# Token rows loaded in a second layout, and the normalizing root moved behind the first projection

## The reference

```
h = rmsnorm(x, g)        # x * rsqrt(mean(x*x) + eps) * g, row by row
z = h @ w_in             # columns [q_a | k_a | v_a | q_b | k_b | v_b | g_b | gate_a | gate_b]
q_b, k_b = rope(q_b), rope(k_b) * DK**-0.5
```

## Time and profile before

| | us |
|---|---|
| median of 3 runs (2119.41 to 2120.04) | 2119.41 |
| the profiled execution | 2120.73 |
| its span, first to last instruction | 2118.9 |
| PE busy / DVE / ACT / POOL | 1940.3 / 1164.1 / 852.5 / 211.5 |
| stage A, tile 0: from the start to the first transposes of q and k | 39.25 |
| stage A, tiles 1 to 8: from there to the same place of tile 8 | 145.12 |

### The profile page before, as it was taken

How to read it: one execution, slowest core, us unless ns; L and a number is a source line. 1 busy time by engine, 2 the same in 40 slices (tenths; PEclk the granted TensorE clock), 3 DMA queues, 4 the chain that set the end, 5 groups by cost and what they waited for, 6 DMA issues and landing times. The chain is left out here.

```text
span 2118.9 us, 26600 instructions
## 1 busy us (share of the span) xinstructions
PE 1940.3 (92%) x9596; PEld 1570.7 (74%) x9596; DVE 1164.1 (55%) x1459; ACT 852.5 (40%) x1018; POOL 211.5 (10%) x222
## 2 busy tenths in 40 slices
PE   6999999974999999997998998689999999999498
PEld 5888888863777777765887786577778777778386
DVE  4234333315333444324444434589999999997574
ACT  4232000011333343324222212477777777776342
POOL 0000111122000000000222000100000000000220
PEclk9999999987999999998999998899999999999699
DMA  8445111187687756584333436589999999997552
GB/s 304 163 154 221 45 57 64 42 295 281 234 309 284 248 177 227 191 290 169 134 128 106 161 110 258 193 323 393 397 396 392 392 391 393 393 397 303 211 193 84
DMA packets 123894, 503.52 MB, mean 238 GB/s; under 512 B 16816, under 2 KB 32688, under 8 KB 101040
## 3 DMA queue, kind: packets, MB, share of 16 engines
q1 hardware_dynamic: 111808, 462.42, 58.5%
q0 software_dynamic: 7200, 26.22, 3.4%
q10 hardware_dynamic: 4816, 13.96, 1.7%
HBM read 407.66 MB, written 94.90 MB: 237 GB/s over the span
## 5 line engine op out<-in xcount | busy, mean ns | idle before, releaser
L2457 DVE TENSOR_TENSOR expert_w_rounded<-arena,expert_w_rounded 128x2048 fp32r<-128x2048 f32 x192 | 430.9, 2284 | 59.5 <-ACT expert_w_rounded L2406 59.5
L2406 ACT ACTIVATE expert_w_rounded<-arena 128x2048 fp32r<-128x2048 f32 x192 | 359.9, 1911 | 47.1 <-PE psum L163 40.0
L161 PE MATMUL psum<-expert_w_rounded,expert_x_rounded 128*128 128x512 f32 x768 | 311.4, 405 | 36.1 <-DVE expert_x_rounded L2470 29.0
L163 PE MATMUL psum<-expert_w_rounded,expert_x_rounded 128*128 128x512 f32 x768 | 302.4, 394 | 0.0
L162 PE MATMUL psum<-expert_w_rounded,expert_x_rounded 128*128 128x512 f32 x768 | 302.0, 393 | 0.0
L161 PEld LDWEIGHTS psum<-expert_w_rounded,expert_x_rounded 128*128 128x128 f32 x768 | 146.4, 191 | 77.1 <-issue 36.2
L161 PE MATMUL psum<-host_w_rounded,host_x_rounded 128*128 128x512 f32 x432 | 182.7, 423 | 8.8 <-DMA host_x_rounded<-hx_scratch 5.8
L163 PE MATMUL psum<-host_w_rounded,host_x_rounded 128*128 128x512 f32 x432 | 171.4, 397 | 0.0
L162 PE MATMUL psum<-host_w_rounded,host_x_rounded 128*128 128x512 f32 x432 | 171.2, 396 | 0.0
L163 PEld LDWEIGHTS psum<-expert_w_rounded,expert_x_rounded 128*128 128x128 f32 x768 | 145.8, 190 | 31.8
L162 PEld LDWEIGHTS psum<-expert_w_rounded,expert_x_rounded 128*128 128x128 f32 x768 | 146.2, 190 | 27.8
(11 more groups left out here) (302 smaller groups left out, 3527.9 us busy)
## 6 DMA issues: line engine op xcount, KB each, us to landing
arena<-w_gate_e SPq DMA_DIRECT2D x32, 2048.0 KB, 9.5
arena<-w_up_e SPq DMA_DIRECT2D x32, 2048.0 KB, 9.6
arena<-w_down_e SPq DMA_DIRECT2D x32, 2048.0 KB, 9.8
host_x_rounded<-hx_scratch SPq DMA_DIRECT2D x54, 1024.0 KB, 5.4
y_scratch<-arena SPq DMA_DIRECT2D x49, 512.0 KB, 10.1
arena<-w_in SPq DMA_DIRECT2D x10, 2048.0 KB, 11.2
z_scratch<-arena SPq DMA_DIRECT2D x54, 256.0 KB, 5.3
arena<-x_all SPq DMA_DIRECT2D x18, 512.0 KB, 4.6
```

Source lines behind the costliest of these rows:

```text
L161: nc.tensor.matmul(out, x_hi, w_hi, start=first, stop=False)
L163: return nc.tensor.matmul(out, x_lo, w_hi, start=False, stop=last)
L2406: nc.scalar.activation(c.exact(his[n][:, half, :]), halves[b][n][:, half, :], ACT.Copy).then_inc(*w_hi_ready[n].inc)
L2457: nc.vector.tensor_tensor(c.exact(raw), raw, c.high(his[n][:, half, :]), ALU.subtract).then_inc(*w_lo_ready[n].inc)
```

## The change

A second copy of the rows, `xT_all`, is laid out on the host with features on partitions. Stage A loads a tile in both layouts. DVE multiplies the transposed tile by g straight into hT (`gained`), without the root; `xn`, its ACT multiplication and PE's `transpose_x` are gone. x itself is only squared. The root is applied where products leave PSUM: as a per-partition scale, read from SBUF, in ACT's copies of q, k and v of branch B, in DVE's copy of v, in the rotation (now one instruction with two multiplications), and in `evict`. POOL makes the root twice in stage A (all nine kept, and a double-buffered one) and copies one number per tile in stage B.

The core of the diff (declarations and address changes left out):

```diff
@@ stage A, POOL and SP
-                nc.gpsimd.tensor_tensor(rstd[:, b:b + 1], ms[:, b:b + 1], c.half[:, 0:1], ALU.pow).then_inc(*rstd_ready.inc)
+                nc.gpsimd.tensor_tensor(rstd[:, t:t + 1], ms[:, b:b + 1], c.half[:, 0:1], ALU.pow).then_inc(*rstd_ready.inc)
+                pool.wait_ge(*k_out(t - 2))
+                pool.wait_ge(*v_out(t - 2))
+                nc.gpsimd.tensor_tensor(row_rstd[:, b:b + 1], ms[:, b:b + 1], c.half[:, 0:1], ALU.pow).then_inc(*rstd_ready.inc)
...
             def load(t, b):
                 if not (isinstance(t, int) and t == 0):
-                    sp.wait_ge(*xn_ready(t - 2))
+                    sp.wait_ge(*hT_ready(t - 2))
+                sp.dma_start(xT[:, b].rearrange("p k n -> p (k n)"), row(c.i["xT_all"], t)).then_inc(*xT_in.inc(b))
+                if not (isinstance(t, int) and t == 0):
+                    sp.wait_ge(*ssq_ready(t - 2))
                 sp.dma_start(x[:, b, :], row(c.i["x_all"], t)).then_inc(*x_in.inc(b))
@@ stage A, ACT
-            def normalize(t, b):
+            def square(t, b):
                 act.wait_ge(*x_in(t, b))
-                act.wait_ge(*xT_done(t - 2))
-
-                nc.scalar.activation(xn[:, b, :], x[:, b, :], ACT.Square, accum_out=ssq[:, b:b + 1]).then_inc(*ssq_ready.inc)
-                act.wait_ge(*rstd_ready(t))
-                nc.scalar.activation(xn[:, b, :], x[:, b, :], ACT.Copy, scale=rstd[:, b:b + 1]).then_inc(*xn_ready.inc)
+                act.wait_ge(*ms_ready(t - 2))
+                nc.scalar.activation(x[:, b, :], x[:, b, :], ACT.Square, accum_out=ssq[:, b:b + 1]).then_inc(*ssq_ready.inc)
...
-                nc.scalar.activation(q, ps[:, 2, :], ACT.Copy).then_inc(*q_out.inc)
+                act.wait_ge(*rstd_ready(t))
+                nc.scalar.activation(q, ps[:, 2, :], ACT.Copy, scale=row_rstd[:, b:b + 1]).then_inc(*q_out.inc)
...
-            normalize(0, 0)
+            hi(0, 0)
             weights_hi([0])
-            hi(0, 0)
+            square(0, 0)
             weights_hi(range(1, 6))
@@ stage A, DVE
+            def gained(t, b):
                 if isinstance(t, int) and t == 0:
                     dve.wait_ge(mix_in, 16)
+                dve.wait_ge(*xT_in(t, b))
+                dve.wait_ge(*lo_ready(t - 2))
                 for h in range(2):
-                    dve.wait_ge(*xT_done(t, h + 1))
-                    if h == 0:
-                        dve.wait_ge(*lo_ready(t - 2))
-                    nc.vector.tensor_tensor(hT[:, b, 4 * h:4 * h + 4, :], ps[:, h, :].rearrange("p (k n) -> p k n", k=4),
+                    nc.vector.tensor_tensor(hT[:, b, 4 * h:4 * h + 4, :], xT[:, b, 4 * h:4 * h + 4, :],
                                             gain(c.g_mix, 4 * h, 4 * h + 4), ALU.mult).then_inc(*hT_ready.inc)
+
+            def mean_square(t, b):
+                dve.wait_ge(*ssq_ready(t))
+                dve.wait_ge(*rstd_ready(t - 2))
+                nc.vector.tensor_scalar(ms[:, b:b + 1], ssq[:, b:b + 1], 1.0 / D, EPS, ALU.mult, ALU.add).then_inc(*ms_ready.inc)
...
-                    h_transposed(t + 1, 1 - b)
+                    gained(t + 1, 1 - b)
+                    mean_square(t + 1, 1 - b)
                     lo(t + 1, 1 - b)
...
-            h_transposed(0, 0)
+            gained(0, 0)
             lo(0, 0)
             weights_lo([0])
+            mean_square(0, 0)
             weights_lo(range(1, 6))
@@ stage A, PE
                 project(t, b, 0)
                 project(t, b, 1)
-                if ahead or t == NT - 2:
-                    transpose_x(t + 1, 1 - b)
                 project(t, b, 2)
...
-            transpose_x(0, 0)
             tile(0, 0, True)
@@ stage B, POOL and DVE
+            def scaled(t, b):
+                pool.wait_ge(*k_read(t - 2))
+                pool.wait_ge(*bv_out(t - 2))
+                nc.gpsimd.tensor_copy(row_rstd[:, b:b + 1], c.rstd[:, ds(t, 1)]).then_inc(*rs_ready.inc)
...
                     t = i * 2 + (1 + b)
+                    scaled(t, 1 - b)
                     project_part(t)
                     retain_part(t - 1)
                     decayed(t)
...
+                dve.wait_ge(*rs_ready(t))
                 for n in range(2):
-                    nc.vector.tensor_tensor(tmp[:, n, :].rearrange("p (h d) -> p h d", h=2 * HB), src,
-                                            rot[:, b, 2 * part + n, :].unsqueeze(1).to_broadcast([P, 2 * HB, DK // 2]),
-                                            ALU.mult).then_inc(*read.inc)
+                    nc.vector.scalar_tensor_tensor(tmp[:, n, :].rearrange("p (h d) -> p h d", h=2 * HB), src, row_rstd[:, b:b + 1],
+                                                   rot[:, b, 2 * part + n, :].unsqueeze(1).to_broadcast([P, 2 * HB, DK // 2]),
+                                                   ALU.mult, ALU.mult).then_inc(*read.inc)
@@ Hosted.evict
-        self.c.nc.scalar.activation(self.zs[:, u % 2], self.c.psum[:, 6 + u % 2, :], ACT.Copy).then_inc(*self.z_out.inc)
+        self.c.nc.scalar.activation(self.zs[:, u % 2], self.c.psum[:, 6 + u % 2, :], ACT.Copy, scale=self.c.rstd[:, u % NT:u % NT + 1]).then_inc(
+            *self.z_out.inc)
```

More of the change, by code:

```diff
@@ L220 @@
 HALF = GAINS + 32
-WORK = HALF + 16
+RSTD = HALF + 16
+WORK = RSTD + 16
 ARENA = 52 * 1024 - 128
@@ L249, in __init__ @@
         self.ident = self.at(IDENT, P)
-        self.half = self.at(HALF, 16)
+        self.half, self.rstd = self.at(HALF, 16), self.at(RSTD, NT)
         self.g_mix, self.g_ffn, self.g_ple, self.g_ret = (self.at(GAINS + 8 * n, KD) for n in range(4))
@@ L350, in stage_ab @@
     c.stages.append(s)
[L351 to L354, removed]
+    x_in, xT_in, hx_stored, k_stored, qz_stored, kT_stored, v_stored = s.dmas(
+        "x_in", "xT_in", "hx_stored", "k_stored", "qz_stored", "kT_stored", "v_stored")
+    ssq_ready, ms_ready, rstd_ready = (s.counter(n, per) for n, per in (("ssq_ready", 1), ("ms_ready", 1), ("rstd_ready", 2)))
+    hT_ready, qz_ready = (s.counter(n, 2) for n in ("hT_ready", "qz_ready"))
     proj_done = s.counter("proj_done", 3)
@@ L361, in stage_ab @@
     tmp = Room(c, R1 + 16 * 1024, R2)
-    x, xn, hT, qz = tmp.take(2, D), tmp.take(2, D), tmp.take(2, KD, P), tmp.take(2, HA, P)
+    x, xT, hT, qz = tmp.take(2, D), tmp.take(2, KD, P), tmp.take(2, KD, P), tmp.take(2, HA, P)
     w, w_hi = c.at(R2, 6, 4 * WA), c.at(R1 + 4 * 1024, 6, 4 * WA)
@@ L366, in stage_ab @@
     q, k, kT = work.take(WA), work.take(2, WA), work.take(2, FA, P)
-    ssq, ms, rstd = work.take(2), work.take(2), work.take(2)
+    ssq, ms, rstd, row_rstd = work.take(2), work.take(2), c.rstd, c.at(RSTD + NT, 2)
     vs = c.at(KV + 8 * 1024, 2, WA)
@@ L379, in stage_ab @@
     state_out, rb_ready = r.counters("state_out", "rb_ready", per=4)
-    norm_steps = r.counter("norm_steps", 8)
+    norm_steps, rs_ready = r.counter("norm_steps", 8), r.counter("rs_ready")
     tables_in, cleared, state_stored = (c.sem(f"b_{n}") for n in ("tables_in", "cleared", "state_stored"))
@@ L523, in tile @@
                 if ahead or t == NT - 2:
-                    normalize(t + 1, 1 - b)
+                    square(t + 1, 1 - b)
                 act.wait_ge(*proj_done(t, 1))
                 act.wait_ge(*qT_done(t - 1))
-                nc.scalar.activation(q, ps[:, 2, :], ACT.Copy).then_inc(*q_out.inc)
+                act.wait_ge(*rstd_ready(t))
+                nc.scalar.activation(q, ps[:, 2, :], ACT.Copy, scale=row_rstd[:, b:b + 1]).then_inc(*q_out.inc)
                 act.wait_ge(*proj_done(t, 2))
                 act.wait_ge(*k_stored(t - 2, b))
-                nc.scalar.activation(k[:, b, :], ps[:, 3, :], ACT.Copy).then_inc(*k_out.inc)
+                nc.scalar.activation(k[:, b, :], ps[:, 3, :], ACT.Copy, scale=row_rstd[:, b:b + 1]).then_inc(*k_out.inc)
                 if ahead or t == NT - 2:
@@ L535, in tile @@
                 if isinstance(t, int) and t == NT - 1:
-                    act.wait_ge(*xT_done(t))
+                    act.wait_ge(*hT_ready(t))
                     panel_hi(act, 1)
-            normalize(0, 0)
+            hi(0, 0)
             weights_hi([0])
-            hi(0, 0)
+            square(0, 0)
             weights_hi(range(1, 6))
@@ L580, in tile @@
                 dve.wait_ge(*v_stored(t - 2, b))
-                nc.vector.tensor_scalar(vs[:, b, :], ps[:, 4, :], 1.0, None, ALU.mult).then_inc(*v_out.inc)
+                dve.wait_ge(*rstd_ready(t))
+                nc.vector.tensor_scalar(vs[:, b, :], ps[:, 4, :], row_rstd[:, b:b + 1], None, ALU.mult).then_inc(*v_out.inc)
                 dve.wait_ge(*qT_done(t))
@@ L605, in _ @@
             pe.wait_ge(ident_in, 16)
-            def transpose_x(t, b):
-                pe.wait_ge(*xn_ready(t))
-                for h in range(2):
-                    pe.wait_ge(*hT_ready(t - 1, h + 1))
-                    for kk in range(4 * h, 4 * h + 4):
```

(13 more changed lines are left out.)

3 lines of the change are left out of this document (removed).

## The result

The changed kernel took 2107.66 us (median of 6 runs), the kernel before 2120.19 beside it: ratio 0.9932, interval 0.9915 to 0.9950. Two repeats, each beside runs of the kernel before on the same chip, gave 0.9938 (0.9913 to 0.9962) and 0.9913 (0.9893 to 0.9932).

What follows compares the result with a forecast made beforehand. PE's instruction list was taken to bound stage A's tiles and stage B; 6.1 (tiles 1 to 7) + 1.0 (tile 0) = 7.1 us off, stages B and C 0, giving 2112.3. Range 2109.5 to 2117.3, the forecast's own 2110.5 to 2114.6.

Steps and rivals of the forecast that it cites:

- the tiles: Stage A, tiles 1 to 7: without transposes of x each takes 17.38 instead of 18.25, 6.1 us off.
- tile 0: Start of stage A: the wait for xn goes, PE's first product comes later; net 1.0 us off.
- stage B: Longer rotations on DVE and POOL's copy lie behind existing waits: 0, at most 3.3 us if that cover were gone.
- The row of tile 8 already is the tile as it will be: Stage A: the old last tile, without transposes of x, took 17.38; tiles 1 to 7 would take the same.
- The gain lands later: Head of tile 0: 0.52 MB more queued ahead delays the gain by 1.36 us, from 10.40 to 11.8.
- The chain behind the landing: Head of tile 0: from the gain's landing to PE's first product 7.5 us instead of 5.7, including a table load of 1.28.
- rival 5: Head of tile 0: the table load also costs about 1.38 us of draining; 5.7 off, 2113.7; chance 0.02.
- Rival 2: Quick head: table loaded before the wait, gain only 0.51 later; 9.2 off, 2110.2; chance 0.10.
- Rival 1: Head takes more: gain 2.3 later, slow clock lasts twice as long; 3.8 off, 2115.6; chance 0.15.
- 3: Stage C: ACT's scale in the evictions costs 4.9 us; 2.2 off in all, 2117.2; chance 0.08.
- 4: Stage C: longer evictions make PE miss one more in each of six panels, 18 us lost; 2130.3, slower; chance 0.05.
- what would show it: Signs expected in the profile: tiles of 17.4, first product at 18.5 to 20, DVE's start near 11.8, evictions of 0.68.

Runs made afterwards that it cites:

- pe_x8: Changed kernel with eight unread transposes of the identity put back on PE between project 1 and 2 of tiles 0 to 7; 2108.78 us, ratio 0.9940.
- pe_x8_2: Repeat of the changed kernel with eight unread identity transposes in each of tiles 0 to 7, beside the changed kernel's 2103.61; 2110.12 us, ratio 0.9946.
- after_back: Changed kernel with the work area back at its address before the change; 2107.23 us, ratio 0.9941.
- table_early: Changed kernel with a one-column ACT copy behind the load of -0.5, so the activation table loads while ACT is idle; 2106.26 us, ratio 0.9926.
- evict_plain: Changed kernel with the 54 hosted evictions of stage C without their scale from SBUF; 2106.07 us, ratio 0.9919.
- rest_moved: Changed kernel with the split rows at their address before the change and everything behind them 64 bytes further; tiles of 17.35 us, no total time given.
- shift: Kernel before the change with only its work area moved 64 bytes further; 2116.53 us, ratio 0.9981.

## Why the prediction missed

**The direction and the main mechanism were right**: PE's list bounds the tiles, and the transposes were its own time (`pe_x8`, `pe_x8_2`). Stage B and C cost nothing, as forecast. The forecast of 7.1 fell short in three terms: the tiles (7.25 for 6.1), tile 0 (3.5 for 1.0) and stage B (0.9 for 0).

**"The row of tile 8 already is the tile as it will be": mis-sized by 0.15 a tile.** It would have been true at the old address: `after_back` has 17.37 in all eight tiles, 138.94, which is 6.2 less than before, the forecast's 6.1. The other 1.1, down to 137.83, is the address, a mechanism that the prediction did not have. At the address that the change gives the split rows, the products stand 0.227 apart instead of 0.229, and the 72 of a tile (3 projects of 24) take about 0.15 less. So tiles 1 to 7 gave 7 x (18.25 - 17.23) = 7.1 and not 6.1, and tile 8, priced at 0, 0.15. That the diff moves an operand by 64 bytes stood there to be read; no row of before told what it does.

**"The gain lands later", 1.36: it did not.** It landed at 10.42, 9.67, 10.49 and 10.33 in four profiles of the changed kernel, at 10.40, 9.92, 10.50 and 9.52 in four of the one before: 0.14 later on the mean. I had set the extra load against a rate as if the rate were full from the start. The DMA rate up to 5 us and from there to the landing, before:

```profile
0.00:5.00 5.00, 0.00 (x0) 0.00 (x0) 0.00 (x0) 1.83 (x2) 0.18 (x4) 1.00 0.51 154
5.00:10.40 5.40, 1.94 (x8) 1.57 (x8) 0.15 (x1) 2.22 (x4) 0.55 (x1) 1.00 0.98 314
```

and after:

```profile
0.00:5.00 5.00, 0.00 (x0) 0.00 (x0) 0.00 (x0) 0.00 (x0) 0.19 (x4) 1.00 0.57 205
5.00:10.40 5.40, 0.00 (x0) 0.00 (x0) 0.00 (x0) 0.00 (x0) 0.00 (x0) 1.00 1.05 335
```

154 x 5 + 314 x 5.4 KB are 2.47 MB, 205 x 5 + 335 x 5.4 are 2.83: some 0.37 of the additional 0.52 MB went in the same time. The other six profiles agree: 146 to 160 GB/s up to 5 us before, 203 to 210 after. Why the queue moves more when a further load stands in it was not tried. The lower bound that I gave, one issue of 0.51, excluded "nothing" on the ground that all which stood ahead stays there; that is true of order, not of rate.

**Tile 0: 3.5 and not 1.0, by the means of four profiles** (39.76 to 36.24). The chain behind the landing was right as a sum: 7.5 forecast, 7.51 measured, the table load bare in it (`table_early`). The drain of rival 5 stayed out of the sum. The trace bears that out: the activation begins 0.01 behind the load's end (11.22 + 1.28, 12.51), and `table_early` gave back 1.27. The Trainium skill ("ScalarE: Activation LUTs", What ACT_TABLE_LOAD costs) adds about 1.38 of draining to every switch to a different set of tables, which no run here shows. The stretch from the first product to the transposes of q, 19.0 forecast, was 19.34, 18.83, 17.99 and 17.85. But the loss that the change takes away was larger than the one profile showed: that stretch took 23.12 in it, and 24.72, 25.18 and 23.62 in the repeats, with waits for `xn` of 4.00, 4.00 and 3.33 for its 3.07, and behind the two of 4.00 the lower clock, on which the forecast put no price at that place. So the start cost 2.1 on the means (15.60 to 17.74) instead of 3.2, and the run behind it gave 5.7 (24.16 to 18.50) instead of 4.1.

**Stage B: 0, measured as a gain of 0.9.** I let PE's 0.39 of idling at its entry stand. Before, PE waits for DVE's low part of a panel:

```profile
202.16 0.47 PE L161 MATMUL psum<-b_w_rounded,b_x_rounded 128*128 128x512 f32 x1 [0.39 <-DVE b_w_rounded L425]
```

After, that wait is not there (PE is busy for 239.90 of 239.90), and the first transposes of stage B come 0.65 sooner behind stage A's end; by the end of stage B it is 0.9, in `after_back` still 0.65, so the other part comes with the address. With the transposes put back (`pe_x8`) the wait returns with 0.59 and the gain is gone. Why the panel is in time without them was not tried. The rotations' 0.061 apiece (2.2 in all; the forecast's 9 x 0.4 = 3.3 is 36 x 0.091) and POOL's copies lie under the 8.26 and 2.87 that DVE waits for PE.

**The sum as measured**: tiles 1 to 7 7.1, tile 8 0.15, tile 0 3.5, stage B 0.9, 11.7 of the 12.9 by which the spans differ on the means, and of the 12.5 by the medians. The rest is not told from the scatter behind stage A.

**The rivals.** None was it. Rival 2, a quick head, was right on the landing and wrong on the table; its 2110.2 is the nearest. Rival 1 is out by the landing and by its clock (14, 12, 7 and 7 slow products at the start for the dozen), 5 by `table_early`, 3 and 4 by `evict_plain` and the single wait of 3.1. The range failed mainly for the head: its bounds were those of one profile, and other profiles of the same kernel move stage A's start by 2.6 us. Of "what would show it", three signs missed on the quick side, DVE's start (10.42 for 11.8), the first product (17.93 for 18.5 to 20) and the tile (17.23 for 17.4). The rest came: the second x at 44.50 without a wait of PE, evictions of 0.68. Tile 8's transposes of q, set at 177.3, came at 175.1.

## What to carry to other kernels

Where an engine is busy in every slot of a stage, count its instructions there, and then look whether the change also moves an operand in memory: a shift of 64 bytes was worth a seventh of the gain in a tile. A load put into a queue that is still starting up may cost its successors nothing; bound it at nothing as well. Price a head from several profiles of the same kernel: tiles repeat to hundredths, heads and late stages by microseconds.

## What the runs showed of the hardware

- The address of the operand that PE loads as weights changes how far apart fp32r products of 128x512 stand; that it is this operand is shown for 0 and 64 bytes (`rest_moved`). From the address before the change on: 0.2288 at 0 bytes, 0.2267 at 64 (in most projects), 0.2334 at 128, 0.2327 at 192 (a mean). A tile of 72 products took 17.37, 17.23, 17.68 and 17.63 (the last a mean of tiles of 17.60 and 17.67). What the steps follow is open.
- 4 KB in single floats, issued at 3.05 behind 1 MB of weights, landed at 10.42; issued ahead of everything, they were no longer what DVE waited for at 5.32.
- The products at the lower clock (0.43 apart) at PE's start were 14, 12, 7 and 7 in four profiles of the changed kernel, under a granted clock given as 1.00.
- Behind an idle of 4.00 in tile 0 PE worked at a granted clock of 0.51 and 0.59 (two profiles of the kernel before), behind 3.07 and 3.33 at 1.00, behind 2.67 in `shift` at 0.59.
